# Hybrid decoder step on one core: the token search with three rounds per tile, and the sample side's values spread over tiles 27 to 34

## What is computed

```python
(q_a, k_a, v_a, g_a, qi, ki, wi, q_c, k_c, v_c, g_c, z, xbc, dt_raw) = project(rms_norm(x, norm_w), w_in)
# sample side of the sparse attention: 2048 cached positions in 16 pages per sequence
sc = indexer_scores(qi, wi, ki_all)                 # (8 seq, 4 tokens, 2052 keys)
_, idx = lax.top_k(sc, 256)                         # the 256 best keys of each token
o_a = sparse_attend(q_a, kvg[..., 0], kvg[..., 1])  # softmax over those keys, 4 heads
# windows with dilation 1, 4, 16 on the last 128, 512, 2048 rows of three caches
o_c, new_bufs = dilated_sample(q_c, k_c, v_c, bufs) # the shifted caches are outputs too
y_b, conv_new, h_new = ssd_branch(z, xbc, dt_raw, conv_state, h0, ...)   # 6 heads, state 128
h = x + concat[o_a * silu(g_a), o_c * silu(g_c), y_b] @ w_out
```

## Time and profile before

| | |
|---|---|
| median of 3 runs | 713.45 us (709.35 to 720.49) |
| the profiled execution | 712.24 us |
| its span, first to last instruction | 710.6 us |
| mean granted clock of PE in it | 0.944 of full speed |
| PE busy | 623.6 us, 88% of the span |
| DVE, POOL, ACT busy | 373.7, 210.5, 171.5 us |
| moved by the transfers | 198.38 MB, mean 279 GB/s |

### The profile page before, as it was taken

The page is one execution under the profiler, slowest core; times in us unless marked ns, Lnnn a source line. Parts: engine busy times, 40 slices in busy tenths (PEclk is TensorE's granted clock), DMA queues, the critical chain, the costliest instruction groups (busy, mean ns, idle before and its releaser), DMA issues.

```text
span 710.6 us, 13795 instructions
## 1 busy us (share of the span) xinstructions
PE 623.6 (88%) x4870; PEld 433.8 (61%) x4870; DVE 373.7 (53%) x1150; ACT 171.5 (24%) x407; POOL 210.5 (30%) x382
## 2 busy tenths in 40 slices
PE   6899999889999877868999999998999977787894
PEld 4666565666677554526777665576677755443673
DVE  3754565577558853114137555676665886312313
ACT  3015222121113143302011342212111314231201
POOL 2207441122115332744000374122211433265000
PEclk9999999989899988879999999999999999988998
DMA  9939999966788694999433799997878979599021
GB/s 338 355 119 324 370 369 409 402 240 255 278 320 302 209 385 146 345 353 318 145 118 122 249 371 367 396 402 271 325 245 322 328 249 381 169 350 335 30 90 66
DMA packets 70838, 198.38 MB, mean 279 GB/s; under 512 B 11537, under 2 KB 44466, under 8 KB 69490
## 3 DMA queue, kind: packets, MB, share of 16 engines
q1 hardware_dynamic: 53138, 99.47, 40.4%
q0 software_dynamic: 17632, 98.03, 37.8%
HBM read 189.30 MB, written 52.00 MB: 340 GB/s over the span
## 4 chain that ended last, share of the span: by engine, by line
PE 54%; DMA 17%; DVE 13%; SPq 6%; issue 6%; ACT 3%; POOL 1%; POOLq 0%; ACTq 0%; DVEq 0%
PE bank L832 51%; DMA kv<-in_kk 8%; DMA kv<-in_vv 5%; SPq L405 5%; PE bank L879 3%; DMA out_p_ssd<-xws 2%; DVE hit L1460 2%; DMA w<-in_w 1%; DVE tb L1473 1%; SPq L401 1%; DVE tb L1471 1%; DMA ptab<-in_ptab 1%; DVE phased L1775 1%; ACT shared L671 1%; DVE phased L1772 1%
## 5 line engine op out<-in xcount | busy, mean ns | idle before, releaser
L832 PE MATMUL bank<-xn,w 128*128 128x288 f32 x1120 | 302.0, 425 | 2.2 <-DMA w<-in_w 2.2
L832 PEld LDWEIGHTS bank<-xn,w 128*128 128x128 f32 x1120 | 213.9, 197 | 73.9 <-issue 13.2
L405 POOL DMA_DIRECT2D kv<-in_kk x128 | 68.8, 538 | 150.3 <-issue 91.0
L405 POOL DMA_DIRECT2D kv<-in_vv x128 | 69.2, 541 | 85.5 <-PE bank L832 68.1
L624 ACT ACTIVATE pt<-bank 128x288 f32<-128x288 f32 x48 | 19.7, 410 | 229.1 <-PE bank L832 229.1
L832 PE MATMUL bank<-pt,w 128*128 128x288 f32 x256 | 64.5, 407 | 0.0
L832 PE MATMUL bank<-kv,phased 128*32 128x256 f32 x512 | 41.1, 439 | 20.9 <-DMA kv<-in_vv 20.9
L832 PEld LDWEIGHTS bank<-pt,w 128*128 128x128 f32 x256 | 48.3, 190 | 13.4 <-issue 0.3
L1460 DVE TENSOR_SCALAR_CACHE_REDUCE hit<-sc,tb 128x516 bf16<-128x516 f32 x62 | 46.5, 750 | 2.2
L508 POOL DMA_DIRECT2D out_keep<-in_buf x48 | 23.8, 500 | 57.9 <-PE bank L832 57.7
L832 PEld LDWEIGHTS bank<-kv,phased 128*32 128x32 f32 x512 | 14.1, 117 | 40.7 <-DMA kv<-in_vv 21.2
(11 more groups left out here) (242 smaller groups left out, 812.1 us busy)
## 6 DMA issues: line engine op xcount, KB each, us to landing
w<-in_w SPq DMA_DIRECT2D x86, 512.0 KB, 5.9
out_keep<-in_buf POOLq DMA_DIRECT2D x16, 2044.0 KB, 11.4
kv<-in_kk SPq DMA_DIRECT2D x128, 160.0 KB, 8.2
kv<-in_kk POOLq DMA_DIRECT2D x128, 160.0 KB, 5.8
kv<-in_vv SPq DMA_DIRECT2D x128, 128.0 KB, 6.0
kv<-in_vv POOLq DMA_DIRECT2D x128, 128.0 KB, 5.6
kv<-in_dil SPq DMA_DIRECT2D x16, 576.0 KB, 10.5
kv<-in_dil POOLq DMA_DIRECT2D x16, 576.0 KB, 7.8
```

Of the source, the lines that this page charges most:

```text
L405: engine.dma_start(kv[:, s, r * rec:(r + 1) * rec], a["kk" if what == "page" else "vv"][bass.ds(page + layer * N_POOL, 1)].rearrange("o p ...
L832: return pe.matmul(out, lhsT, rhs, start=start, stop=stop, skip_group_check=True, **k)
```

## The change

Nothing in the arithmetic changes; instructions are moved, and four buffers get another place.

1. `proj(i, *counts)` takes up to three rounds: after the third, the sixth and the eighth matmul of a tile. Rounds 0 to 29 stand in tiles 16 to 25, 30 and 31 in tile 26. DVE's work between rounds is dealt out anew, at most one piece to a round, and the top-8 rounds, the windows' scores and the states' sums come after the search.
2. The eight `window_keys`, the ties and the mask stand after tile 26, the exponential and its transposes after tile 27 and the first two state sums.
3. Page values are spread: groups 0 to 3 ahead of tile 28, 4 and 5 ahead of 29, one after each of the eight window values around tile 30, 14 to 31 around tiles 32 to 34. `RING` has the same order, and SP's and POOL's lists follow it. The sum `so` is in bank 4 and begins with group 0; the new tokens' part is added after tile 33.
4. `sct` lies in 9 slots of `pt` that the index keys, the queries and the convolution leave free (so `QA` and `XBC` change places), no longer in the states' buffer; ACT waits for the index keys' transfer (`ki_out`) instead of the states', which it now awaits at the layer's end. `cum` and `pns` move into `ea`.
5. The `keep` copies are issued at tiles 16, 17, 18, 19, 20, 21, 23 and 24.
6. ACT copies `cbs` after tile 19, behind the decays' exponential.

```diff
-RING = ([("page", n) for n in range(KITEMS)] + [("window", n) for n in range(2 * NB)] + [("value", n) for n in range(NGRP)])
+RING = ([("page", n) for n in range(KITEMS)] + [("window", n) for n in range(NB)] + [("value", n) for n in range(6)]
+        + [(kind, n + (NB if kind == "window" else 6)) for n in range(NB) for kind in ("window", "value")]
+        + [("value", n) for n in range(6 + NB, NGRP)])
...
-        sct = phased[:, 0:NPG, :]
+        sct = pt[:, SLOTS[KI]:SLOTS[XBC] + NXBC, :].rearrange("p a n -> p (a n)")[:, 0:NPG * P].rearrange("p (j n) -> p j n", n=P)
...
+                for i, (lo, hi) in enumerate(((32, 40), (40, 44), (44, 46), (46, 54), (54, 62), (62, 66), (66, 70), (70, 74))):
+                    consumed(*RING[lo:hi])
+                    next_w(27 + i)
+                consumed(*RING[74:])
...
-                act.wait_ge(filled("cbs"), nth(L, "cbs"))
-                act.activation(cbs[:, :], bank_of("cbs")[0:32, 0:64], ACT.Copy).then_inc(drained("cbs"), 1)
                 act.wait_ge(S["adt_ready"], nth(L, "adt_ready", 1))
...
-                act.wait_ge(S["h_out"], nth(L, "h_out", 32))
...
-                def proj(i, mid_count=None, end_count=None):
+                def proj(i, *counts):
+                    at = {len(counts): (3, 7)[:len(counts)], 3: (2, 5, 7)}[len(counts)]
...
-                        if k == 3 and mid_count is not None:
-                            bit_count(mid_count)
+                        if k in at and k < KT - 1:
+                            bit_count(counts[at.index(k)])
...
                 for h in range(6):
-                    proj(21 + h, 10 + 2 * h, 11 + 2 * h)
+                    proj(21 + h, *range(15 + 3 * h, min(18 + 3 * h, BITS + 1)))
                     head(h)
-                    if h >= 2:
-                        window_keys(2 * h - 4)
-                        window_keys(2 * h - 3)
...
-                window_values(0)
-                window_values(1)
-                bit_count(28)
+                for b in range(4):
+                    window_values(b)
+                    value_group(6 + b)
+                proj(30)
...
                 compare(16)
-                rope(13)
+                g_mul(0)
+                lin(1)
                 settle(16)
                 compare(17)
-                lin(4)
-                g_mul(3)
+                rope(10)
                 settle(17)
```

More of the change, by code:

```diff
@@ L173, in bank_plan @@
             use(f"y{h // 2}", 7)
[L174 to L178, removed]
[5 rows of a table removed]
+    for name, bank in (("dk", 6), ("msk0", 2), ("msk1", 3), ("msk2", 5), ("msk3", 4), ("msk4", 7), ("dnt", 7), ("ss0", 3), ("ss1", 5),
[6 rows of a table added]
                        ("sot", 3)):
@@ L745, in _ @@
                 evac(19)
+                act.wait_ge(filled("cbs"), nth(L, "cbs"))
+                act.activation(cbs[:, :], bank_of("cbs")[0:32, 0:64], ACT.Copy).then_inc(drained("cbs"), 1)
                 act.wait_ge(filled("st0"), nth(L, "st0"))
@@ L1907, in _ @@
-                g_mul(4)
+                g_mul(1)
+                lin(2)
                 settle(19)
                 compare(20)
-                top8_round(1)
+                rope(11)
                 settle(20)
                 compare(21)
-                g_mul(5)
+                y_out(0)
                 settle(21)
                 compare(22)
-                window_scores()
-                y_out(2)
+                g_mul(2)
+                lin(3)
                 settle(22)
                 compare(23)
-                top8_round(1)
@@ L1941, in _ @@
[L1941 removed]
+                y_out(1)
                 settle(27)
                 compare(28)
[L1945 to L1946 removed]
+                g_mul(4)
+                lin(5)
                 settle(28)
                 compare(29)
[L1949 to L1950 removed]
                 settle(29)
                 compare(30)
[L1954 removed]
+                rope(13)
                 settle(30)
                 compare(31)
[L1957 removed]
+                g_mul(5)
@@ L1991, in _ @@
                 ts_(st4[:, 1:2], st4[:, 0:1], -1.0, None, ALU.mult).then_inc(S["sexp_in"], 1)
+                window_scores()
+                state_out(0)
+                state_out(1)
+                dve.wait_ge(S["sexp"], nth(L, "sexp", 1))
+                tt_(xn4[:, :].rearrange("p (b k) -> p b k", b=NB), mid(srow[:, NPG * P:], NB),
+                       C("dsel").rearrange("p (b k) -> p b k", b=NB), ALU.mult).then_inc(S["px_ready"], 1)
+                dve.reciprocal(st4[:, 3:4], st4[:, 2:3]).then_inc(chain.next(), 1)
+                dve.wait_ge(S["dve_chain"], chain.n)
+                window_probs()
+                top8_round(1)
+                top8_round(1)
+                state_out(2)
+                state_out(3)
+                prompt_state_out()
+                top8_round(1)
+                top8_round(1)
+                top8_round(1)
+                state_out(4)
+                state_out(5)
+                top8_round(1)
+                top8_round(1)
+                top8_round(1)
+                state_out(6)
+                state_out(7)
+                prompt_mask(1)
+                inverse_group(0)
+                inverse_group(2)
                 group_normed()
```

308 lines of the change are left out of this document (133 added, 175 removed), and 11 rows, old and new, of the table uses.

## The result

The changed kernel takes 685.86 us (median, 685.09 to 689.4), the kernel before 716.97 us in the same comparison: a ratio of 0.961, interval 0.956 to 0.966. Medians are over all runs of a kernel, ratios over its fast runs alone, so a ratio is not always the quotient of two medians. The forecast was 684, the range 664 to 708. The profiled execution took 685.09 us with a span of 683.4, 27.2 us less than the 710.6 of before.

What follows compares the result with a forecast made beforehand. PE's own work filled three quarters of the changed region, the rest waiting and slow clock. Per layer 154.5 + 15 + 9.5 + 2 + 10 = 191 us, against 207.8 and 202.6, gave 684 us, range 664 to 708.

Steps and rivals of the forecast that it cites:

- waits for the search: Tiles 16 to 26: PE waits for search rounds longer than the matmuls between sums, 15 us a layer.
- mask, exponential, transposes, tail: After the search: PE waits for mask and exponential, `sct` copies, dilated probabilities and last transposes, 9.5 us a layer.
- waits for values: Page values, mostly around tile 30: 2 us a layer, bounds 0 and 10; POOL's issuing pace kept it from 0.
- clock: From tile 16 to the first output tile: 10 us a layer lost to the lower clock, between 2 and 15.4.
- work at full clock: From tile 16 to the first output tile: PE's busy time less clock loss, unchanged at 154.5 us a layer.
- The third the round less 1.03 us: Third sum of a three-round tile: PE waits the round less two matmuls, 1.45 us in tiles 21 to 25.
- I cost it at nothing: Cache copies in tiles 16 to 21: a transfer queue of some 10 us builds up but costs PE nothing.
- The cover that I named: POOL's next loads are wanted only near 215 us, after the last copy; failing that, odd ring items are late.
- Rival A: Only long waits cost clock: clock term 2 instead of 10 us a layer, 668 us in all; chance 0.14.
- Rival C: Search holds PE's clock near 0.7 in tiles 16 to 26: 22 us more a layer, 728 us; chance 0.06.
- Rival B: Transfers still bound; value waits move to tile 30 and groups 14 to 25, 10 us a layer: 706 us; chance 0.18.
- signs of a wrong forecast: Value or window waits over 8 us a layer in tiles 28 to 34, clock under 0.8, weight waits beside copies.

Runs made afterwards that it cites:

- a7: Changed kernel with ring order window, value, value, window around tile 30, so both queues share the values: 690.6 us, ratio 0.962 to the kernel before.
- a4: Changed kernel without the eight cache copies of each layer: 688.72 us, ratio 0.962 to the kernel before.
- b2: Kernel before with only the cache copies issued early: 719.69 us, ratio 1.007 to the kernel before.
- a2: Changed kernel with the cache copies back at tiles 16, 18, 20, 22, 24, 26, 28 and 30: 716.97 us, ratio 1.007 to the kernel before.
- a3: Changed kernel without the 32 search rounds (compare, sums, settling): 692.98 us, ratio 0.969 to the kernel before.
- a5: Changed kernel with DVE's pieces moved to search rounds that a head or three matmuls hide: 683.0 us, ratio 0.954 to the kernel before.
- a6: Changed kernel with the prompt's first transposes and second dots ahead of tile 34: 677.89 us, ratio 0.946 to the kernel before.
- b1: Kernel before with only `sct` moved into `pt`, ACT waiting for the index keys' transfer: 713.31 us, ratio 0.996 to the kernel before.
- a1: Changed kernel with all window items again ahead of the page values and all 32 value groups after tile 33: 710.91 us, ratio 0.995 to the kernel before.

## Why the prediction was right

The sum for a layer was 191 us from the windows' starts of the earlier trace rows, which is 192.1 and 192.2 from the first matmul of tile 16. It came to 193.46 and 193.39. Its terms, with layer 0 from the rows (all waits of PE from 116.36 to 309.82 added up) where not said otherwise:

| term | forecast | measured |
|---|---|---|
| waits for the search | 15 | 9.8 (eleven waits); 18.8 + 0.7 us for both layers |
| mask, exponential, transposes, tail | 9.5 | 6.6 |
| waits for values | 2 | 5.3; layer 1 6.0 |
| waits for weights | 0 | 1.3 |
| clock | 10 | 11.6 (0.06 x 193.46); layer 1 13.5 (0.07 x 193.39) |
| work at full clock | 154.5 | 158.5; layer 1 157.4 (busy less clock) |

So the total is right within 1.4 us, but partly by compensation, which is luck: the idle terms (26.5 us forecast, 23.0 measured) were 3.5 us too high, the clock 1.6 us too low, and the work 2.9 us, once the 1.1 us of the later window's start are added to it; the clock's rounding to 0.01 is 1.9 us of the last two's split.

*The work.* The step "175.4 - 22.9 = 152.5" is why it was too low. The same matmuls, cut at the same instructions and worked out the same way, give 153.4 and 157.7 us for the two layers before and 158.5 and 157.4 after: layer 0 of before is the odd one. The granted clock is a mean over the window, idle time included, so 0.11 of the window's length also takes off clock that was low while PE stood still. That would explain it; no run separates it from rounding.

*The search* was the term sized worst. "The third the round less 1.03 us": the two matmuls ahead of the third sum took 1.22 us (162.53), not 1.03, so the wait is 1.28 us and not 1.45. Two of the five third rounds in tiles 21 to 25 (0.32 and 0.91 us) were covered in part by PE's own slower matmuls, and the 0.09 us of the second sums show nowhere. The mechanism was right: the eleven waits stand at the eleven places named, and only the twelfth, 0.5 us in tile 26, is missing.

*Mask, exponential, transposes.* 1.2 us forecast, 0.68 measured; the copies into `sct` 1.5 against 0.65; the dilated turns 1.3 against 0.40; the last transposes 4.0 against 3.96.

*The values.* "I allow 2 us a layer" was too little: 5.3 and 6.0, inside the bounds of 0 and 10. The step that was mis-sized is the time from issue to use of the window and value items around tile 30. The transfers are at 0.95 there. The reason that kept me from taking 0, POOL's pace of issuing, is not the cause by a7, and the early copies are not by a4 (12.9 us without them).

*The copies.* The step "I cost it at nothing" holds in the changed kernel, where a4 shows no price in the time; it wasn't quite nothing, since PE waits 1.3 us for weights in layer 0 and b2 has 7.4 us more of such waits than before, at 1.007 (1.000 to 1.013). But I didn't see what they are worth: with the copies late, the spread values lose all their gain (a2). The cover that I named, POOL's next loads are wanted only when the last copy is through, is what the change rests on: in a2, where copies stand among those loads, it costs 33 us.

*The clock.* Rival A, that only long waits cost clock, is refuted by the three-matmul groups at 168.39 and by a4's 0.92. The Trainium skill, TensorE: Matmul & The Clock Gate, section "HAM oscillation — how this bites in real kernels", lays the fall to long idle gaps; the tiles of 7.1 and 7.0 us behind waits of 2.9 and 4.0 us in a3 agree with it. The 3.25 us at 168.39 do not: no wait in the 50 us ahead of them was longer than 1.73 us. Rival C needed 0.79 in tiles 16 to 26; it is 0.92, the same as before. Rival B needed 10 us of value waits and 20 of clock a layer; its place was right (the dense stretch around tile 30), its size half.

Of the three things that the text named as signs of a wrong forecast, two stayed away (values under 8 us a layer, clock over 0.8) and one came: PE waits for weights beside the copies, 1.3 us at tile 26 of layer 0. It was a nearer thing than it looks: a3 and a5 show the weights about level with the search. Of the signs for the single steps, three missed: the compare's waits in tiles 21 to 25 were 0.3 to 1.3 us and not 1.4 to 1.6, those for values 5.3 and 6.0 and not under 3, and 0.25 us for `lim` were left in each layer. The region's length, the states' transfer, the clock and the last transposes came as named.

## What to carry to other kernels

Where a ring of buffers feeds an engine, spread the uses over the other work, and keep big copies, on whatever queue, out of the stretch in which the ring is filled: here, with either of the two edits taken back, next to nothing of the gain was left (0.995 and 1.007 against 0.961). Before an engine's waits are trimmed, look at the transfers' share in the same stretch: here, at 0.96 to 0.98, the next limit was right behind, and waits taken away came back under another name (a3, and in part a5). A wait near the end of a stage, with only finished operands around it, was a better target (a6, 11 us) than one in a stretch that the transfers fill (a5, 5 us that the noise can hide, for 8 us of waits removed).

## What of the hardware I had not expected

- A copy from memory to memory costs its issuing engine 1.5 us, and yet with such copies among the ring's loads PE waited up to 7.6 us for values and 5.8 us for a window, and the loads of the other queue, SP's, landed late too (8.2 us against 5.1, a2).
- The weights' landing follows the load on the transfers, though they go by SP's queue and the copies by POOL's: by the transfers' share in tiles 16 to 26 of layer 0, the median is 3.8 us at 0.30 (a4), 5.9 at 0.74 (a2) and 0.81 (before), 6.8 at 0.84 (b1), and 7.2 to 7.7 at 0.96 to 1.00 (a3, a1, the changed kernel, b2).
- PE's clock fell where no wait had been longer than 1.73 us (3.25 us for what takes 1.70), and the slower work then hid a part of the next wait (0.32 us instead of 1.28), so the two losses are not additive.
